# Encoder trunk with a two-layer mixture of experts: last down matrices in row chunks, with a scatter of their own for the eighth duo

## The reference

```python
h = h + hier_moe(rms_norm(h, ln_ffn[layer]), ...)       # at the end of each of 2 layers
for gi in range(MOE_GROUPS):                             # 4 groups x 4 experts, 1024 -> 512 -> 1024
    hid = silu(einsum('td,edf->tef', t, w_gate[gi])) * einsum('td,edf->tef', t, w_up[gi])
    hid = hid * gate[:, gi, :, None]
    y = y + einsum('tef,efd->td', hid, w_down[gi])
...
return rms_norm(h, ln_final)
```

## Time and profile before

| | us |
|---|---|
| median of 3 runs | 1030.85 (1027.38 to 1037.57) |
| profiled execution | 1031.11 |
| its span, first to last instruction | 1029.3 |
| PE busy | 980.1 (95%) |
| DVE, ACT busy | 267.5 (26%), 196.5 (19%) |
| weight queue's packets, share of 16 engines | 74.0% |
| layer 0's last scatter ends | 434.89 |
| layer 1's last scatter ends | 1019.93 |

### The profile page before, as it was taken

The page is one execution under the profiler, slowest core; times in us unless marked ns, Lnnn a source line. Parts: engine busy times, 40 slices in busy tenths (PEclk is TensorE's granted clock), DMA queues, the critical chain, the costliest instruction groups (busy, mean ns, idle before and its releaser), DMA issues.

```text
span 1029.3 us, 10800 instructions
## 1 busy us (share of the span) xinstructions
PE 980.1 (95%) x4388; PEld 575.4 (56%) x4388; DVE 267.5 (26%) x655; ACT 196.5 (19%) x383; POOL 11.1 (1%) x21
## 2 busy tenths in 40 slices
PE   7999999999899998999999999999999898999995
PEld 5578468444243433488778877877475443434331
DVE  3334333331112111422202220221244311121115
ACT  3005312132111210301111110110122221212102
POOL 1110000000000000000000000000000000000000
PEclk9999999999999999999999999999999899999999
DMA  9793272369999989998193491688162699999993
GB/s 343 271 356 117 99 297 100 146 237 413 428 429 427 413 368 422 345 239 226 15 288 96 86 280 32 153 292 350 59 241 98 251 417 429 428 429 379 431 411 141
DMA packets 118484, 282.50 MB, mean 274 GB/s; under 512 B 4631, under 2 KB 82791, under 8 KB 107177
## 3 DMA queue, kind: packets, MB, share of 16 engines
q1 hardware_dynamic: 116992, 278.18, 74.0%
q0 software_dynamic: 1168, 3.40, 1.0%
q10 hardware_dynamic: 280, 0.31, 0.1%
HBM read 280.76 MB, written 1.11 MB: 274 GB/s over the span
## 4 chain that ended last, share of the span: by engine, by line
PE 85%; DMA 10%; DVE 3%; issue 1%; SPq 1%; ACT 0%; DVEq 0%
PE banks L1158 80%; DMA ring<-expert_w_up_in 6%; PE banks L1161 3%; DMA ring<-expert_w_down_in 3%; PE banks L1532 2%; SPq L613 1%; DMA scratch<-mem_in 1%; DVE h L1878 0%; ACT nrm L907 0%; DVE h L1870 0%; DVE mx L1994 0%; DVE nrm L1945 0%; DVE nrm L2002 0%; DVE late L759 0%; ACT late L757 0%
## 5 line engine op out<-in xcount | busy, mean ns | idle before, releaser
L1158 PE MATMUL banks<-ring,scratch 128*64 128x512 f32 (+1 forms) x1696 | 439.5, 597 | 19.6 <-DMA ring<-expert_w_up_in 9.8
L1158 PEld LDWEIGHTS banks<-ring,scratch 128*64 128x64 f32 (+1 forms) x1696 | 153.7, 145 | 268.3 <-issue 261.9
L1158 PE MATMUL banks<-late,ring 128*128 128x256 f32 x1040 | 227.2, 379 | 1.1 <-DVE late L759 0.6
L1158 PEld LDWEIGHTS banks<-late,ring 128*128 128x128 f32 x1040 | 196.5, 190 | 28.2 <-issue 1.9
L862 ACT ACTIVATE scratch<-banks 128x512 f32<-128x512 f32 (+4 forms) x100 | 66.7, 685 | 395.2 <-PE banks L1161 294.9
L1158 PE MATMUL banks<-ring,late 128*128 128x384 f32 (+2 forms) x320 | 102.7, 476 | 0.0
L2247 DVE TENSOR_SCALAR scratch<-banks 32x1024 f32<-32x1024 f32 x28 | 34.2, 1222 | 207.2 <-PE banks L1158 207.0
L1158 PEld LDWEIGHTS banks<-ring,late 128*128 128x128 f32 x320 | 57.4, 190 | 37.7 <-issue 7.7
L1158 PE MATMUL banks<-scratch 128*128 128x128 f32 (+5 forms) x388 | 78.1, 369 | 0.0
L1158 PEld LDWEIGHTS banks<-scratch 128*128 128x128 f32 (+2 forms) x388 | 48.5, 177 | 29.3 <-issue 21.5
L2225 DVE TENSOR_TENSOR scratch<-banks,scratch 128x512 f32<-128x512 f32 x16 | 16.9, 1058 | 120.3 <-PE banks L1158 120.3
(11 more groups left out here) (157 smaller groups left out, 439.6 us busy)
## 6 DMA issues: line engine op xcount, KB each, us to landing
ring<-expert_w_up_in SPq DMA_DIRECT2D x24, 2048.0 KB, 14.2
ring<-expert_w_gate_in SPq DMA_DIRECT2D x22, 2048.0 KB, 13.9
ring<-expert_w_down_in SPq DMA_DIRECT2D x20, 2048.0 KB, 13.1
ring<-odd_w_in_in SPq DMA_DIRECT2D x72, 512.0 KB, 7.3
ring<-expert_w_down_in SPq DMA_DIRECT2D x16, 1024.0 KB, 15.1
ring<-xkv_w_in SPq DMA_DIRECT2D x4, 2048.0 KB, 11.6
scratch<-expert_w_gate_in SPq DMA_DIRECT2D x4, 2048.0 KB, 12.7
ring<-expert_w_down_in SPq DMA_DIRECT2D x16, 512.0 KB, 8.0
```

Of the source, the lines that this page charges most:

```text
L1158: return giving_back(nc.tensor.matmul(dst, lhsT, rhs, start=start, stop=stop))
```

## The change

The last pair of down matrices lands in four row chunks in place of two column halves, with a semaphore for each of the first three. PE works duo 7's down chunk by chunk, left and right columns in turn. After chunk 0 it waits for duo 6's rows and runs four scatter calls with `scat` and `ysb` (whose selectors for duo 7 are set to zero), leaving the sums open in the banks. Duo 7's outputs are copied as two whole blocks of 128 rows, left half by ACT and right half by DVE, into `last_rows` (space of the gathered tokens), and four more scatter calls with selectors of their own (`last_scat`) close the sums. `own` holds these selectors with the slots of the other tile set to zero; DVE makes it in `gate_selectors`, PE turns it in two more pieces (`selU`) at q = 6, ACT copies them. The banks of the last sums are 4, 1, 2, 3 in place of 1, 2, 3, 0, and the scratch grows by 608 columns.

```diff
@@ SyncE
-                for pair, first in ((MATRICES - 6, up_half), (MATRICES - 4, next_half), (MATRICES - 2, down_half)):
+                for pair, first in ((MATRICES - 6, [up_half]), (MATRICES - 4, [next_half]), (MATRICES - 2, down_chunk)):
                     if pair == MATRICES - 2:
                         second_pass(l)
-                    for n in range(2):
+                    parts = len(first) + 1
+                    for n in range(parts):
                         for m in (pair, pair + 1):
                             k = ring_index(l, m)
                             if n == 0:
                                 sp.wait_ge(ring_used, k - RING + 1)
-                            dst, src = by_half(m, n)
-                            sp.dma_start(dst, src).then_inc(landed[k % RING] if n else first, 16)
+                            dst, src = by_part(m, n, parts)
+                            sp.dma_start(dst, src).then_inc(landed[k % RING] if n == parts - 1 else first[n], 16)
@@ ScalarE
                     if q == DUOS - 2:
                         second_pass(l, flag)
+                        for t in range(TILES):
+                            k = PIECES[f"selU{l}{t}"]
+                            piece_in(act, k)
+                            copy(last_scat[:, t, :], pbank(k)[:, 0:P]).then_inc(evac[k % 2], 1)
@@
                 act.wait_ge(y_half, l + 1)
-                for i in range(2):
-                    last = copy(*expert_columns(i, 0, 0))
-                last.then_inc(y_act, 1)
-                act.wait_ge(y_ps, (l + 1) * DUOS)
-                for i in range(2):
-                    last = copy(*expert_columns(i, 0, 1))
-                last.then_inc(y_act, 1)
+                copy(*last_columns(0)).then_inc(y_act, 1)
@@ TensorE
                 def last_down_products():
                     q = DUOS - 1
                     m = PLACE["down", q]
-                    pe.wait_ge(down_half, 32 * (l + 1))
                     pe.wait_ge(hT_sb, l * DUOS + q + 1)
-                    for f in range(2):
-                        if f:
-                            last.then_inc(y_half, 1)
+                    for c in range(FC):
+                        if c < FC - 1:
+                            pe.wait_ge(down_chunk[c], 32 * (l + 1))
+                        else:
                             matrix_in(pe, l, m)
                             matrix_in(pe, l, m + 1)
-                        for c in range(FC):
+                        for f in range(2):
                             last = down_part(q, f, c, LAST_DOWN, last_hidT)
+                            if c == FC - 1 and f == 0:
+                                last.then_inc(y_half, 1)
+                        if c == 0:
+                            pe.wait_ge(y_act, of_duo(l, q))
+                            pe.wait_ge(y_dve, of_duo(l, q))
+                            piece_out(pe, f"selT{l}{GROUPS - 1}")
+                            for i in range(4):
+                                t, half = by_columns(i)
+                                mm(bank[MOE_BANK[i]][:, :], scat[:, t, :], ysb[:, t, half * 512:(half + 1) * 512], True, False)
                     last.then_inc(y_ps, 1)
@@
                         if q == DUOS - 2:
                             second_pass(l, flag)
+                            for t in range(TILES):
+                                k = f"selU{l}{t}"
+                                piece_free(pe, k)
+                                flip(pbank(k)[:, 0:P], own[:, t].rearrange("p e n s -> p (e n s)")).then_inc(piece_ready, 1)
@@
                     if t == 0:
-                        pe.wait_ge(y_act, of_duo(l, DUOS - 1) + 1 + f)
-                        pe.wait_ge(y_dve, of_duo(l, DUOS - 1) + 1 + f)
-                    for cols in ((slice(0, 256), slice(256, 512)) if i == 0 else (slice(0, 512),)):
-                        last = mm(bank[MOE_BANK[i]][:, cols], scat[:, t, :], ysb[:, t, f * 512:(f + 1) * 512][:, cols], True, True)
-                    last.then_inc(proj, 1)
+                        pe.wait_ge((y_act, y_dve)[f], (l + 1) * DUOS)
+                    if i == 0:
+                        for n in range(TILES):
+                            piece_out(pe, f"selU{l}{n}")
+                    nc.tensor.matmul(bank[MOE_BANK[i]][:, :], last_scat[:, t, :], last_rows[:, f * 512:(f + 1) * 512],
+                                     start=False, stop=True).then_inc(proj, 1)
@@ VectorE
+                    by = gates[:, :, g].unsqueeze(3).to_broadcast([P, TILES, EPG, SHARE])
+                    if g < GROUPS - 1:
+                        v.tensor_tensor(cols, cols, by, ALU.mult).then_inc(gated_set, 1)
+                        return
+                    for t in range(TILES):
+                        v.memset(own[:, t, :, 1 - t, :], 0.0)
+                        step(v.tensor_tensor(own[:, t, :, t, :], cols[:, t, 2:4], by[:, t, 2:4], ALU.mult))
+                    v.tensor_tensor(cols[:, :, 0:2], cols[:, :, 0:2], by[:, :, 0:2], ALU.mult)
+                    v.memset(cols[:, :, 2:4], 0.0).then_inc(gated_set, 1)
@@
-                dve.wait_ge(y_half, l + 1)
-                for i in range(2):
-                    last = v.tensor_copy(*expert_columns(i, 1, 0))
-                last.then_inc(y_dve, 1)
                 dve.wait_ge(y_ps, (l + 1) * DUOS)
-                for i in range(2):
-                    last = v.tensor_copy(*expert_columns(i, 1, 1))
-                last.then_inc(y_dve, 1)
+                v.tensor_copy(*last_columns(1)).then_inc(y_dve, 1)
```

More of the change, by code:

```diff
@@ L57 @@
 SPAN = 512
-SCRATCH = 18176
+SCRATCH = 18784
 REACH = 260
@@ L224, in encoder @@
         selr, gselr, scatr = (sel[:, 0, n * P:(n + 1) * P] for n in range(3))
+        own = a.take(TILES * P).rearrange("p (t e n s) -> p t e n s", t=TILES, e=2, n=TILES)
+        last_scat = a.take(TILES * P).rearrange("p (t q) -> p t q", t=TILES)
+        last_rows = xg[:, 1].rearrange("p c s -> p (c s)")[:, 0:D]
         kcur = a.take(TILES)
@@ L271, in encoder @@
         next_half = sem("first_chunks_of_next_to_last_down_matrices_landed")
-        down_half = sem("left_columns_of_last_down_matrices_landed")
+        down_chunk = [sem(f"chunk{c}_of_last_down_matrices_landed") for c in range(FC - 1)]
         mem_in = sem("mem_loaded")
@@ L420, in of_duo @@
         def of_duo(l, q):
-            return l * (DUOS + 1) + q
+            return l * DUOS + q
         def closes_group(q):
@@ L437, in number_moe @@
                     number(*[f"gather{l}{g + 1}{j}" for j in range(4)])
+            number(*[f"selU{l}{t}" for t in range(TILES)])
         number_moe(0)
@@ L477, in encoder @@
         E_BANK = (6, 7, 0, 1)
-        MOE_BANK = (1, 2, 3, 0)
+        MOE_BANK = (4, 1, 2, 3)
         LAST_DOWN = (5, 0)
@@ L594, in experts, with by_part @@
                         load_expert(l, m, ring_index(l, m) - W_MOE[l] - RING)
[L596 to L602, removed]
-                for pair, first in ((MATRICES - 6, up_half), (MATRICES - 4, next_half), (MATRICES - 2, down_half)):
+                def by_part(m, n, parts):
+                    rows = slice(n * SLOT // parts, (n + 1) * SLOT // parts)
+                    return matrix(l, m)[:, rows], rows_of(m)[:, rows]
+                for pair, first in ((MATRICES - 6, [up_half]), (MATRICES - 4, [next_half]), (MATRICES - 2, down_chunk)):
                     if pair == MATRICES - 2:
                         second_pass(l)
-                    for n in range(2):
+                    parts = len(first) + 1
+                    for n in range(parts):
                         for m in (pair, pair + 1):
@@ L770, in by_tile, with last_columns @@
             return cols.rearrange("p (e t s) -> p t e s", t=TILES, e=EPG)
-        def expert_columns(i, t, f):
-            to, at, cols = SHARE * (2 + i), SLOTS * i + SHARE * t, slice(f * 512, (f + 1) * 512)
-            return ysb[to:to + SHARE, t, cols], bank[LAST_DOWN[f]][at:at + SHARE, :]
+        def last_columns(f):
+            return last_rows[:, f * 512:(f + 1) * 512], bank[LAST_DOWN[f]][:, :]
         def expert_rows(half, i, t):
@@ L2215, in gate_selectors @@
                     cols = sel[:, :, P * g:P * (g + 1)].rearrange("p t (e s) -> p t e s", e=EPG)
-                    v.tensor_tensor(cols, cols, gates[:, :, g].unsqueeze(3).to_broadcast([P, TILES, EPG, SHARE]),
-                                    ALU.mult).then_inc(gated_set, 1)
+                    by = gates[:, :, g].unsqueeze(3).to_broadcast([P, TILES, EPG, SHARE])
[7 more added lines that the diff above has]
+                    v.memset(cols[:, :, 2:4], 0.0).then_inc(gated_set, 1)
                 def hidden(q):
```

## The result

| | before | after |
|---|---|---|
| median of 20 runs each, us | 1033.81 (1027.38 to 1038.26) | 1040.70 (1036.22 to 1045.31) |
| ratio, with 95% interval | | 1.0068 (1.0050 to 1.0085) |
| ratio, measured again beside 29 runs of before | | 1.0053 (1.0026 to 1.0080) |
| span of the profiled execution, us | 1029.3 | 1036.7 |

The changed kernel is slower by 0.5 to 0.7%, some 5.5 to 7 us; in this case's terms, no change over 1%. The ratio was forecast at 1.0054. The forecast time of 1036.5 us was made against a median of 1030.85; over 20 runs the kernel before itself has 1033.81, which is 3.0 of the 4.2 us by which the changed kernel lies over the forecast.

A forecast was written before the change was run, and what follows sets the result against it. With the change PE, not the landing of the last weights, was to set each layer's end; layer 0's +4.34 us and layer 1's +1.28 us summed to +5.6 us, giving 1036.5 us, range 1031 to 1042.

The forecast's parts named there:

- What bounds: End of each layer's experts: landings set layer 1's end before, 3.3 us of PE idle; after the change PE alone does.
- Part 1, second set: Scatter calls behind chunk 0: doubled, not moved, 3.58 us more PE work per layer, plus waiting for duo 6's row copies.
- Part 2, landing: Last down matrices landing in quarter chunks: four more issues on SP's queue cost nothing; 2.6 us each if uncovered.
- Part 3, copies: Duo 7's output copies: one of 128 rows replaces two of 32, 0.60 us ScalarE, 0.69 VectorE, next to nothing gained.
- Part 4, selectors: Two extra selector turns at q = 6 wait for banks: products start 0.86 us late, bounds 0.41 and 1.5.
- Sum: Whole run: layer 0 +4.34 us, layer 1 +1.28 us, together +5.6 us, giving 1036.5 us; chance 0.74.
- Rival (a): Layer ends: landings stay the bound and the shorter tail gains 1.8 us in each layer, 1027.2 us; chance 0.03.
- Rival (b): Layer 0's 1.88 us PE stall moves: it vanishes, 1034.6 us, or layer 1 gets one too, 1038.4; chance 0.13.
- Rival (c): Between layers: layer 0's 4.3 us are swallowed before the end, only layer 1's +1.3 stays, 1032.1 us; chance 0.10.
- Signs: PE's timeline: no down-matrix wait behind duo 6, about 1 us for rows, gate products 0.9 us later, layer ends 4 and 5.6.
- signs of being wrong: Weight wait before chunk 3, scatter calls under 0.86 us, layer 0 under 3 us later, or layer 1's distance from it shrunk.

The follow-up runs named there:

- chunks alone: Kernel before with only the last down matrices landed and worked in four row chunks, old copies, one set of scatter calls; ratio to before 1.0003.
- no first set: Changed kernel without the first set of four scatter calls, duo 6's part of the last group left out, all waits kept; ratio to before 0.9993.
- set behind chunk 1: Changed kernel with the first set of scatter calls moved from behind chunk 0 to behind chunk 1, same work; ratio to before 1.0036.
- after again: The changed kernel profiled once more with no edit; span 1038.8 us, stretches 41.44 and 38.67 us.
- turns in one bank: Changed kernel with the eighth duo's own selectors turned into the free half of the same bank as the others; ratio to before 1.0047.

## Why the prediction came out right, step by step

- **What bounds.** Right. The prediction's argument was that chunks 0 to 2 and the second set have to fit between duo 6's end and the last landing, and do not. After, in layer 1, PE takes 9.9 us for them, its wait included (1012.00 to 1021.88; 9.8 forecast), and the last landing is in after some 5.4 (about 1017.4). No wait for down matrices is left; moving the set (40.40 and 37.72 us) and leaving it out (3.60 us in layer 1) show PE as the bound.
- **Part 1, second set.** Forecast 3.58 us and 1.0 us of waiting for rows; measured 3.60 and 0.91 (the two executions without this wait, or without the set, are 0.95 and 3.60 shorter). The row names ScalarE as releaser, but its copies ended at 1014.18; VectorE's, 1012.14 + 2.46, ended at 1014.60, 0.1 before PE went on. The last one to finish is the one that was waited for:

```profile
1012.14 2.04 ACT L862 ACTIVATE scratch<-banks 32x1024 f32<-32x1024 f32 x2 [3.02 <-PE banks L1156]
...
1012.14 2.46 DVE L2266 TENSOR_SCALAR scratch<-banks 32x1024 f32<-32x1024 f32 x2 [6.53 <-PE banks L1156]
...
1022.86 0.60 ACT L862 ACTIVATE scratch<-banks 128x512 f32<-128x512 f32 x1 [8.68 <-PE banks L1156]
...
1023.75 0.69 DVE L2271 COPY scratch<-banks 128x512 f32<-128x512 f32 x1 [9.15 <-PE banks L1156]
```

- **Part 2, landing.** No cost of it is seen, as forecast, and the last pair moved faster, at 408 GB/s from 1008 to 1015 where the earlier trace rows has 387. Its landing came some 28.8 us behind the first turn, before 30.1. It helped nobody, as said.
- **Part 3, copies.** Right: the last two rows of the fence, 0.60 and 0.69 us as priced, the first over at 1023.46, ahead of the last set at 1023.60. The second is over at 1024.44, about 0.9 us before the third call, not the 1.72 us that the prediction has. The price of the old copies, 0.72 us of wait in chunks alone, belongs to the order by chunk; that the two larger copies avoid it was not counted as a gain, since the kernel before does not have that order. No run has these copies alone.
- **Part 4, selectors.** The term that was most mis-sized: 0.86 us forecast, 0.59 and 0.62 measured (1.14 us from first turn to first product, against 0.55 and 0.52). The second wait was over 0.1 us sooner than forecast (0.77 us behind the first turn, 0.86 forecast). The rest is that I carried over 0.52 us from first turn to product as if it were the price of two turns. It holds the branch too: in the kernel before without it the product follows after 0.34 us. In the changed kernel the branch adds nothing behind the wait for the bank (1.14 us with it and without it), so it must not be counted there. VectorE's six operations took 0.9 us of the 2.5 allowed.
- **Sum.** Layer 0 +4.34 forecast, +4.39 measured; 0.23 of it is a longer stall (6.29 us against 6.06 for the same 16 records), which fills the gap that part 4 left: that these two agree so closely is luck. Layer 1 +1.28 forecast, +1.13 measured: 0.24 less for the selectors, 0.1 more for the last set (3.70 us; 3.60 forecast). The two are 5.6 and 5.5 us. The time of 1036.5 us missed by 4.2, of which 3.0 are the base of three runs.
- **Rival (a)** is what happens when the second set is left away: chunks alone give 1.4 us in layer 1. **Rival (b)**: the stall stayed where it was. **Rival (c)**: no sign that layer 0's +4.4 us were swallowed, and no proof from the traces either. From its last scatter to layer 1's first turn are 982.39 − 434.89 = 547.50 us before, 548.65 after, but 546.46 in the second profile of the same kernel; the nine profiles have 545.41 to 550.71. The runs speak against it: with layer 1's 1.1 us alone the ratio would be 1.001, below both intervals.
- **Signs.** PE's ends came 5.1 us (layer 0) and 7.4 us (layer 1) later in the first profile, where 4 and 5.6 were named; the difference is 0.70 and then 1.9 us of work outside the stretches. The eighth gate products started 0.6 us later behind the first turn, not 0.9. Of the signs of being wrong one came close, a shorter distance between the layers: from end to end of the last scatters it is 585.04 us before and 587.32 after, but 585.13 in the second profile, where 1.3 more was forecast; up to layer 1's first turn it did shrink there, by 1.0. Two profiles of one kernel differ by 2.2 us in it, which makes it a poor sign.

## What to carry to other kernels

Idle time in front of a landing (the arrival of the data that PE waits for) is only worth filling if the filler fits between the last work and that landing; work that is doubled to shorten the tail is paid in full once it does not fit, and then every stall and every wait for a copy that the landing had covered is paid as well. Lay the sum out to the last landing on the clock of the trace, per layer: the same edit cost 1.1 us where PE had 3.3 us of waits and 4.4 us where it had 0.9. Two profiles of one program can differ by 4 us in code that the edit never touches, so compare stretches between two marks, not spans.

## What the runs showed of the hardware

- Behind a PE stall of about 2 us the granted TensorE clock fell in some profiles and not in others. After 1.86 us of it (no first set) it was 0.50, the lower level of 1.2 GHz, from 404 to 406; after 2.29 us (chunks alone) it was 0.50 from 405 to 407; from 408 on both had 1.00, 2.4 GHz. The 64 records behind the stall took 15.60 and 15.65 us. After 1.88, 2.04, 2.07, 2.14 and 2.27 us (before, set behind chunk 1, after, after again, turns in one bank) they took 13.95 at 1.00. That is 1.7 us in one place, and there are more such places in the program; the length of the stall alone does not decide, and what does is not shown.
- A pass of 32 rows over a bank's 512 columns costs VectorE what one of 128 rows costs: 1.40 us for two before, 0.69 us for one after.
- Weights in rows of 2, of 4 and of 8 or more KB moved at 387, 408 and 421 GB/s, each in one stretch of one trace (before 1001 to 1009, after 1008 to 1015, before 986 to 997).
